# A decoder trunk in fp32 on one core: the first RMS statistics taken from x during the modulation, and a root of a constant ahead of the last squares at three borders

## What is computed

```python
def rms_norm(x, gain):
    y = xf * lax.rsqrt(jnp.mean(xf * xf, axis=-1, keepdims=True) + EPS)
    return (y * gain.astype(jnp.float32)).astype(x.dtype)

def adaln(c, w, b, n):
    m = jax.nn.silu(c) @ w + b
    return jnp.split(m[:, None, :], n, axis=-1)

def modulate(x, gain, shift, scale):
    return rms_norm(x, gain) * (1 + scale) + shift

for layer in range(DEPTH):
    if layer == N_A_LAYERS:
        shared_kv = nsa_shared_kv(x, c, kv_gain, kv_mod_w, kv_mod_b, w_kv, ...)
    sh1, sc1, g1, sh2, sc2, g2 = adaln(c, mod_w[layer], mod_b[layer], N_MOD)
    h = modulate(x, norm_gain[layer, 0], sh1, sc1)
    y = chunked_sgu(h, ...) if layer < N_A_LAYERS else nsa_attention(h, shared_kv, ...)
    x = x + g1 * y
    h = modulate(x, norm_gain[layer, 1], sh2, sc2)
    x = x + g2 * conv_ffn(h, ...)
```

## Time and profile before

| | before |
|---|---|
| median of 3 runs | 2656.17 us (2649.58 to 2662.58) |
| profiled execution | 2656.14 us |
| its span, first to last instruction | 2654.4 us |
| mean granted TensorE clock | 0.977 of full speed |
| TensorE busy | 2543.2 us, 96% |
| VectorE busy | 2147.4 us, 81% |
| ScalarE busy | 1243.2 us, 47% |
| GpSimd busy | 406.2 us, 15% |
| moved by DMA | 685.47 MB, 258 GB/s on average |

### The profile page before, as it was taken

How to read it: one execution, slowest core, us unless ns; L and a number is a source line. 1 busy time by engine, 2 the same in 40 slices (tenths; PEclk the granted TensorE clock), 3 DMA queues, 4 the chain that set the end, 5 groups by cost and what they waited for, 6 DMA issues and landing times.

```text
span 2654.4 us, 38453 instructions
## 1 busy us (share of the span) xinstructions
PE 2543.2 (96%) x13984; PEld 2185.0 (82%) x13984; DVE 2147.4 (81%) x2569; ACT 1243.2 (47%) x1638; POOL 406.2 (15%) x217
## 2 busy tenths in 40 slices
PE   3789999998999999999998999999899999999999
PEld 2668888887888888888887879788788888888887
DVE  7967898899989888988999886687999756665666
ACT  2245443444555355534544444483455435543553
POOL 4000020123111011101132300172212001100110
PEclk9899999999999999999999988899999999999999
DMA  7979688887777977787766876306677655555543
GB/s 295 372 296 355 254 328 329 319 324 269 277 284 277 352 272 287 278 336 278 278 254 246 312 297 268 149 1 244 246 297 280 244 182 187 186 189 183 189 174 143
DMA packets 94310, 685.47 MB, mean 258 GB/s; under 512 B 10465, under 2 KB 10465, under 8 KB 11233
## 3 DMA queue, kind: packets, MB, share of 16 engines
q1 hardware_dynamic: 93746, 681.27, 68.3%
q10 hardware_dynamic: 432, 2.38, 0.2%
HBM read 681.51 MB, written 2.10 MB: 258 GB/s over the span
## 4 chain that ended last, share of the span: by engine, by line
PE 86%; DVE 6%; DMA 3%; ACT 1%; issue 1%; POOL 1%; SPq 0%; DVEq 0%; ACTq 0%; POOLq 0%
PE banks L1406 51%; PE banks L1408 26%; DMA raw<-in_stream 3%; DVE raw L1054 2%; DVE w_lo L1038 2%; PE banks L1375 2%; PE banks L1378 2%; PE banks L1377 2%; PE banks L759 1%; DVE temp L1102 1%; ACT w_hi L887 1%; PE banks L1395 1%; PE banks L723 1%; PE banks L745 1%; DVE scratch L829 1%
## 5 line engine op out<-in xcount | busy, mean ns | idle before, releaser
L1038 DVE TENSOR_TENSOR w_lo<-raw,w_hi 128x1024 fp32r<-128x1024 f32 x841 | 1088.4, 1317 | 362.6 <-ACT w_hi L887 358.7
L1406 PE MATMUL banks<-h_op,w_hi 128*128 128x512 f32 x3840 | 1359.3, 399 | 21.6 <-DVE h_op L1108 18.2
L887 ACT ACTIVATE w_hi<-raw 128x1024 fp32r<-128x1024 f32 x841 | 876.2, 1056 | 1031.9 <-PE banks L1408 638.9
L1408 PE MATMUL banks<-h_op,w_lo 128*128 128x256 f32 x3840 | 1080.7, 281 | 0.0
L1406 PEld LDWEIGHTS banks<-h_op,w_hi 128*128 128x128 f32 x3840 | 724.3, 189 | 200.8 <-issue 22.8
L1406 PE MATMUL banks<-act_op,w_hi 128*128 128x512 f32 x2176 | 769.8, 399 | 0.0
L1408 PEld LDWEIGHTS banks<-h_op,w_lo 128*128 128x128 f32 x3840 | 729.1, 190 | 0.0
L1408 PE MATMUL banks<-act_op,w_lo 128*128 128x256 f32 x2176 | 611.6, 281 | 0.0
L1054 DVE CUSTOM_DVE_ANT_0 raw<-raw,c_all 128x2048 f32<-128x2048 f32 x224 | 558.8, 2515 | 14.4 <-ACT c_all L873 9.6
L1406 PEld LDWEIGHTS banks<-act_op,w_hi 128*128 128x128 f32 x2176 | 409.5, 188 | 102.1 <-issue 0.8
L1408 PEld LDWEIGHTS banks<-act_op,w_lo 128*128 128x128 f32 x2176 | 411.8, 189 | 0.0
(11 more groups left out here) (151 smaller groups left out, 1395.8 us busy)
## 6 DMA issues: line engine op xcount, KB each, us to landing
raw<-in_stream SPq DMA_DIRECT2D x645, 1024.0 KB, 5.4
x_res<-in_x SPq DMA_DIRECT2D x1, 2048.0 KB, 11.3
out_x<-x_res SPq DMA_DIRECT2D x4, 512.0 KB, 5.0
mix_area<-in_w_s ACTq DMA_DIRECT2D x1, 1024.0 KB, 4.9
mix_area<-in_b_s ACTq DMA_DIRECT2D x1, 1024.0 KB, 8.2
small<-in_small SPq DMA_DIRECT2D x1, 682.0 KB, 16.2
attn_area<-in_pos ACTq DMA_DIRECT2D x1, 273.0 KB, 5.4
c_all<-in_c SPq DMA_DIRECT2D x1, 8.0 KB
```

Source lines behind the costliest of these rows:

```text
L887: act.activation(w_hi[:, out, 0:n], raw[:, slot, half:half + n], ACT.Copy).then_inc(hi_ready, 1)
L1038: dve.tensor_tensor(w_lo[:, out, 0:n], raw[:, slot, half:half + n], w_hi[:, out, 0:n].bitcast(F32), ALU.subtract).then_inc(stream, 2 if ch ...
L1406: pe.matmul(banks[:, g + j, :], hi[:, k, P * j:P * (j + 1)], operand[:, kt, :], start=(kt == 0), stop=False, skip_group_check=True)
L1408: last = pe.matmul(banks[:, g + j, 0:T], lo[:, k, P * j:P * (j + 1)], operand[:, kt, 0:T], start=False, stop=(kt == last_kt), skip_group_c ...
```

## The change

GpSimd no longer squares x for the head. Instead ScalarE, right after silu(c), squares all four quarters of x, 128x1024 each, into the two halves of `temp` in turn; TensorE, right after spreading c, adds each with four matmuls of ones into bank 0, 16 in all. ScalarE then takes the root. The reciprocal on VectorE moves from behind the modulation vectors to between the sixth and the seventh modulation piece. From the head's `make_h` the squares and the root are gone. At the three later borders ScalarE takes a root of the constant eps into a new tile of 128x1 ahead of its wait for GpSimd and of the four squares; the semaphore counts of the three remaining calls are one call lower.

```diff
@@ -873,6 +876,18 @@
             act.activation(c_all[:, :].rearrange("p (b n) -> p b n", b=4), banks[:, 4:8, :], ACT.Silu) \
                 .then_inc(c_ready, 1)
 
+            act.wait_ge(x_loaded, 16)
+            for q in range(QUARTERS):
+
+                if q >= 2:
+                    act.wait_ge(x_squares_read, q - 1)
+                act.activation(temp[:, q % 2, :], x[:, TPC * q:TPC * (q + 1), :].rearrange("p k t -> p (k t)"),
+                               ACT.Square).then_inc(x_squared, 1)
+            act.wait_ge(summed, 1)
+            act.wait_ge(consts_set, 1)
+            act.activation(rstd[:, :], banks[:, 0, 0:T], ACT.Sqrt, scale=1.0 / D, bias=eps[:, :]) \
+                .then_inc(rms_ok, 1)
+
...
@@ -889,15 +904,13 @@
             def make_h(name, tiles, fresh, ready):
 
                 i = h_index(name)
-                if fresh:
+                if fresh and name != "head":
                     k = STAT_ORDER.index(name)
-                    if k == 0:
-                        act.wait_ge(x_loaded, 16)
-                    act.wait_ge(xhalf, 3 * (k + 1))
+                    act.wait_ge(consts_set, 1)
+                    act.activation(root_probe[:, :], eps[:, :], ACT.Sqrt)
+                    act.wait_ge(xhalf, 3 * k)
                     for j in range(TPC):
-                        if k:
-
-                            act.wait_ge(xlow, TPC * BY_NAME[X_FROM[name]][3].n["xup"] + j + 1)
+                        act.wait_ge(xlow, TPC * BY_NAME[X_FROM[name]][3].n["xup"] + j + 1)
                         act.activation(y4[:, j, :], x[:, 3 * TPC + j, :], ACT.Square).then_inc(squared, 1)
                     act.wait_ge(summed, k + 1)
                     act.wait_ge(consts_set, 1)
@@ -1081,14 +1094,19 @@
                     dve.scalar_tensor_tensor(out=out, in0=out, scalar=1.0, in1=small[:, g:g + n], op0=ALU.add,
                                              op1=ALU.mult).then_inc(mod_ready, 1)
 
+            def invert_rms(k):
+
+                dve.wait_ge(rms_ok, k + 1)
+                dve.reciprocal(rstd[:, :], rstd[:, :]).then_inc(rstd_ok, 1)
+
             def make_h(name, tiles, fresh, ready):
 
                 i = h_index(name)
                 shift, scale, _ = H_OF[name]
                 if fresh:
                     k = STAT_ORDER.index(name)
-                    dve.wait_ge(rms_ok, k + 1)
-                    dve.reciprocal(rstd[:, :], rstd[:, :]).then_inc(rstd_ok, 1)
+                    if k:
+                        invert_rms(k)
                     dve.wait_ge(rstd_ok, k + 1)
                 dve.wait_ge(mod_ready, ready)
                 if name == "q":
@@ -1187,6 +1205,8 @@
                     elif t == "m":
                         mod_piece(cur, m, tok)
                         m += 1
+                        if name == "head" and first and m == 6:
+                            invert_rms(0)
...
                 if q == 3:
                     return
-                n = 3 * k + q
-                if k == 0:
-                    pool.wait_ge(x_loaded, 16)
-                else:
-                    name = STAT_ORDER[k]
-                    pool.wait_ge(xlow, TPC * (BY_NAME[X_FROM[name]][q].n["xup"] + 1))
+                n = 3 * (k - 1) + q
+                name = STAT_ORDER[k]
+                pool.wait_ge(xlow, TPC * (BY_NAME[X_FROM[name]][q].n["xup"] + 1))
                 tiles = x[:, TPC * q:TPC * (q + 1), :].rearrange("p k t -> p (k t)")
                 if n:
                     pool.wait_ge(xhalf, n)
@@ -1244,9 +1261,6 @@
                     pool.tensor_copy(gt[:, 0:256], gt[:, 256:512]).then_inc(xsum, 1)
                 else:
                     pool.tensor_tensor(gt[:, 0:256], gt[:, 0:256], gt[:, 256:512], ALU.add).then_inc(xsum, 1)
-
-            for q in range(3):
-                sum_squares(0, q)
 
...
@@ -1328,6 +1342,12 @@
                 spread = pe.matmul(banks[:, 4 + b, :], ones[0:1, :], c_all[0:1, 512 * b:512 * (b + 1)], start=True,
                                    stop=True)
             spread.then_inc(c_spread, 1)
+            for q in range(QUARTERS):
+                pe.wait_ge(x_squared, q + 1)
+                for j in range(TPC):
+                    last = pe.matmul(banks[:, 0, 0:T], ones[:, :], temp[:, q % 2, T * j:T * (j + 1)],
+                                     start=(q == 0 and j == 0), stop=(q == QUARTERS - 1 and j == TPC - 1))
+                last.then_inc(summed if q == QUARTERS - 1 else x_squares_read, 1)
 
             def step(name, cur, prev, first):
                 kind = cur.first.kind
@@ -1337,14 +1357,13 @@
                 free_wait(pe, cur)
                 if name == "sgu_u0" and cur.first.loc == 1:
                     mix_pe(g)
-                if first and name in H_OF and H_OF[name][2]:
+                if first and name in H_OF and H_OF[name][2] and name != "head":
 
                     k = STAT_ORDER.index(name)
-                    pe.wait_ge(consts_set, 1)
-                    pe.wait_ge(xsum, 3 * (k + 1))
+                    pe.wait_ge(xsum, 3 * k)
                     pe.matmul(banks[:, 0, 0:T], ones[:, :], gt[:, 0:T], start=True, stop=False)
                     for j in range(TPC):
-                        pe.wait_ge(squared, TPC * k + j + 1)
+                        pe.wait_ge(squared, TPC * (k - 1) + j + 1)
                         last = pe.matmul(banks[:, 0, 0:T], ones[:, :], y[:, T * j:T * (j + 1)], start=False,
                                          stop=(j == TPC - 1))
                     last.then_inc(summed, 1)
```

More of the change, by code:

```diff
@@ L311, in build @@
         eps = sb("eps", [P, 1])
+        root_probe = sb("root_probe", [P, 1])
         banks = ctx.enter_context(nc.psum_tensor("banks", [P, 8, 512], F32))
@@ L354, in build @@
         mod_ready = sem("mod_ready")
+        x_squared = sem("x_squared")
+        x_squares_read = sem("x_squares_read")
         xsq = sem("xsq")
```

## The result

The changed kernel takes 2639.03 us as the median of 6 runs (2634.20 to 2640.96), beside 2655.27 us for the kernel before on the same chip. The two medians lie 16.2 us apart. The ratio is formed over the single executions and not from the medians: it is 0.9934 with a 95% interval of 0.9915 to 0.9953, which is 17.5 us less, or between 12.5 and 22.6. The profiled execution took 2635.02 us, near the short end of the six. The forecast was 14.7 less, 2641.4 us.

A forecast was written before the change was run, and what follows sets the result against it. TensorE, busy 96%, was taken as the bound, apart from the head's hole and the three borders. Head 14.2 us plus borders 0.5 made 14.7, so 2656.14 - 14.7 = 2641.4 us; range 2635 to 2650.

The forecast's parts named there:

- What the hole is made of: Head, before 55 us: TensorE idle or partly used, waiting on GpSimd's squares, sum, root and reciprocal; first norm at 48.50.
- The squares on ScalarE and the sum on TensorE: Head: quarter 0 summed at 17.9 us, the whole sum at 27.8, or about 25; root at 28.3 or 25.5.
- a clock that rises meanwhile: Head's sum on TensorE: the last matmuls run faster, sum complete at about 25 us instead of 27.8.
- The rival of a late root: Head: reciprocal waits in VectorE's queue, each microsecond from 27.3 us costs one; price 4.0, time 2645.4 us; chance 0.06.
- VectorE's pieces: Head: pieces shorter without GpSimd, piece 6 done at 27.3 us, first norm at 34.1 instead of 48.50, 14.4 earlier.
- The stream does not give it back: Transfers after the head's hole: between 13.5 and 14.4 us of the shift survive to the end, 14.2 taken.
- transfers at 3.0 us a piece: Rival, head: transfers bound it at 3.0 us steps, not 2.5; shift 12.3 or 11.3, time 2643.3 to 2645; chance 0.22.
- quarters more than 34 us apart: Sign of being wrong: the head's quarters start more than 34 us apart, against 33.8 in the kernel before.
- The roots of a constant: Part 2, three later borders: table load moved ahead of the squares, covered by idle time; gain 0.5 us, bounds -0.3 and 1.5.
- there the gain is nothing: Second and third border: the root waits for TensorE's matmuls after the table load, so moving the load gains nothing.
- the 0.5%: What a measurement of this kernel can tell from no change, 13.3 us; the forecast lay 1.4 us beyond it.
- The rival that ends slower: After the head: TensorE stays at half clock 30 us longer, costing 15 us, 2656.3; slower by over 0.5% has chance 0.02.

The follow-up runs named there:

- the repetition: The changed kernel measured once more, with no edit; median 2640.78 us beside 2654.85 for the kernel before, ratio 0.9944.
- probes_only: The kernel before plus only the root of a constant at the three later borders; 2653.10 us beside 2652.24 for the kernel before, ratio 1.0008.
- head_only: The changed kernel without the root of a constant at the three borders; 2638.36 us beside 2652.24 for the kernel before, ratio 0.9951.
- pool_busy: The changed kernel with GpSimd still squaring and folding three quarters of x, result unread; 2645.69 us beside 2652.24 for the kernel before, ratio 0.9974.
- x_first: The changed kernel with x transferred ahead of pieces 1 and 2 and the reciprocal behind the fourth modulation piece; 2642.68 us, ratio 0.9953 to the kernel before.

## Why the prediction was right, point by point

- **What the hole is made of.** Right. With the wait gone the hole closed, and TensorE's busy time stayed the same.
- **The squares on ScalarE and the sum on TensorE.** The order of events was right, the size too cautious. Quarter 0 was summed near 18.2 (17.9 as worked out). But the twelve matmuls after it took 5.2 us, 0.43 each, where the first four had taken about 0.9, so that the sum was complete at 23.5, and not at 25 to 27.8. The prediction had named the case, a clock that rises meanwhile, and put the rise too late: the first clock record, at 18.2 us, has full clock, and the change of pace lies there, after TensorE had added for 3.8 us. It made no difference, since VectorE comes to the reciprocal at 27.24. The rival of a late root had 3.3 us of room, and the run with the doubled sum shows that it costs one for one at the first norm once that room is used up.
- **VectorE's pieces.** Right to 0.1 us: reciprocal at 27.24 (27.3), first norm at 34.02 (34.1). One premise was wrong and did no harm: the landings of before were kept since the DMA engines were full, but pieces 7 and 8 landed at 27.4 and 29.9 instead of 28.7 and 31.2. The reciprocal stands there, and VectorE comes to piece 8 only at 31.1, when it would have landed in either case. The prediction put the first norm's 14.4 us down in one sum. The runs split it: 8.3 us of waiting for the statistics and 6.15 of GpSimd's contention with VectorE, of which 2.6 lie in the modulation vectors.
- **The stream does not give it back.** Right. The shifts at the four quarters are 14.48, 13.73, 13.91 and 14.25 us, and the value taken was 14.2. The last figure is nearer than one profile can promise: the repetition has 15.55 there, and probes_only, with the head of before, starts its last quarter 1.1 us ahead of the kernel before. The slot of piece 9 was refilled by an issue at 40.1 (40.2). It landed at 44.9, sooner than the 45.7 of the prediction, since piece 12 had landed at 39.9 and not at 43.2. Then the next two steps took 3.4 and 3.0 us and not 2.5, so that piece 15 landed at 51.2 (50.7): two errors that partly cancel. The rival, transfers at 3.0 us a piece, rested on the pace of landings before. In the changed kernel pieces 5 to 12 came 2.5 us apart, and it fell. Steps of 3.0 to 3.9 us came for three pieces after 44.9 us, without GpSimd; in the repetition they were 2.5, 3.3 and 3.8. The second quarter was 0.75 us short of the first in the first profile and 0.1 in the repetition. What makes those steps was not found. By a sign that the prediction had named for being wrong, quarters more than 34 us apart, the first profile is over the line, 34.5 us from the first quarter to the second, and the repetition is not, 33.8.
- **The roots of a constant.** The mechanism and the cover were right, the size was off: the step "there the gain is nothing" for borders 2 and 3. It was read from one execution in which TensorE ran the last of those matmuls at 1.2 GHz at two of the three borders (granted clock 0.50 in 1405.0 to 1405.6 us at the second). The stretch around the third border, before and after:

```profile
1894.00:1899.00 5.00, 3.56 (x8) 1.77 (x8) 2.27 (x6) 3.40 (x6) 0.00 (x0) 0.67 0.49 200
```

```profile
1872.00:1876.00 4.00, 2.53 (x8) 1.23 (x8) 2.21 (x6) 2.11 (x5) 0.00 (x0) 1.00 0.55 221
```

  The granted clock is 0.67 of full in the one and 1.00 in the other. At full clock the load ends last at all three borders, as head_only shows, and moving it is worth 0.48 us at each, 1.45 in all, the upper bound that the prediction gave. Where the clock falls during the matmuls it is worth nothing. That can hit any border: in the eight profiled kernels that have no load behind the squares, the root starts 2.86 to 3.15 us after the first square at 18 of 24 borders, and 3.6 to 4.2 us at the other six, where the granted clock of the stretch is 0.61 to 0.85. Before it was 3.74 and 4.09 at 0.82 and 0.70. The kernels' medians cannot tell 0.5 from 1.5.
- **The size of the whole.** 14.7 us forecast; by rows 14.25 + 1.45 = 15.7, or 15.55 + 1.45 = 17.0 with the repetition's head; measured 16.2 and 14.1 by the medians of the two groups, 17.5 and 14.9 by the ratios. That 14.7 lies so near is in part luck, since two profiles of the same code differ by more than its terms were off. Both ratios lie beyond the 0.5% (0.66 and 0.56%), but both intervals reach over that line, to 0.47 and 0.40%, as near as the forecast had put it.
- **The clock after the head.** The rival that ends slower did not come: the mean granted clock is 0.979 and 0.977 in the two profiles, 0.977 before.

## What to carry to other kernels

An engine that is "free" is not free if its work lengthens that of the engine that sets the pace: here 6 of 14.5 us came from stopping the work on GpSimd, and only the rest from having the result earlier. One run with the same work, for nobody, tells the two apart. When a wait at the start of a stream is removed, follow the slots that it kept full: here the gain survived because the first refill was issued earlier by the same amount (40.1 instead of 54.6 us). And a term that is read as "hidden behind TensorE" at one border needs the granted clock beside it, since the same border at full clock may leave it bare.

## What the runs showed of the hardware that was not expected

- VectorE's product of 128x2048 takes 2.29 us alone and 2.47 to 3.98 beside GpSimd's squares and folds, and its products and sums of 128x4 columns together, with the gaps between them, 3.13 us instead of 0.56 (pool_busy beside the changed kernel).
- Full DMA engines do not move the same bytes at all times. In 24 to 34 us it was 369 to 374 GB/s in three kernels with GpSimd squaring and folding, 414 to 424 in eight without, at the same share of busy DMA engines (0.96 to 1.02). The Trainium skill's page "SBUF — State Buffer", section "Who interferes with whom", says that DMA never contends with a compute engine. These runs don't decide it: the stretch of 24 to 34 us speaks against it, while in 16 to 24 us GpSimd's work changed nothing (422 to 427 GB/s beside 422 to 426), and x_first fell to 336 in 44 to 48 us with GpSimd idle.
- The load of an activation table costs 1.28 us and no more: with two of them in a row on the path the next instruction starts 0.01 to 0.02 us behind each. The Trainium skill's page "ScalarE: Activation LUTs", section "What ACT_TABLE_LOAD costs", adds a drain of about as much again; no run here shows one on the path.
- A stretch of some 750 us differs by 6 us between two executions of the same kernel, at the same granted clock of 1.00. Two single profiled spans, 21.2 us apart here, overstated the change by 5 to 7 us (16.2 and 14.1 by medians).
